# Expert rows taken one by one instead of in pairs, in a fused eight-block model kernel on one Trainium2 core

## Chip, cores and metric

One core of a Trainium2 chip runs the whole program in one launch. The metric is device time in microseconds (us), median of several runs. Three runs of the kernel before gave 3692.46, 3696.25 and 3700.17 us.

## The reference, cut to what matters

Three layers run on 512 tokens of width 1024, all in float32: a short-convolution mixer with a feed-forward part, a state-space mixer with a feed-forward part, and a hybrid layer (band attention beside a gated delta rule) that ends in a retrieval of single-neuron experts. The change concerns that retrieval alone. For each token, eight heads choose 16 of 16384 experts each, so 128 experts per token:

```python
u = expert_down[experts]              # 128 rows of 1024 per token
vv = expert_up[experts]
act = gelu(einsum("thkd,td->thk", u, hb))
out = einsum("thk,thkd->td", gates * act, vv)
```

## The kernel before

**Stages.** The first two layers and the first half (tokens 0 to 255) of the hybrid layer run first. Then the expert stage begins for the four chunks c = 0 to 3 of 128 tokens. While the experts of chunks 0 and 1 are worked on, the second half (f = 1) of the hybrid layer is computed beside them on the same engines, since chunks 2 and 3 need it.

**An expert row.** Tokens lie on the 128 partitions. "Row" n (n = 128c + s, 512 in all) is the s-th expert of each of the chunk's 128 tokens: one gather brings 128 x 2048 floats, 1 MB: `expert_down` in the left half and `expert_up` in the right half. `pool_gather` issues it on GpSimd's queue into a slot of `SLOTS`, after the row that had the slot before has been added (`added(prev[n])`). There are 7 slots (`NRING`) for rows 0 to 255 and 12 from there on, when memory of the finished hybrid layer is added.

**What is done with it.** Rows go in groups of `GG` = 2. `dve_dots` (VectorE, profile line L187) forms the dot with the tokens for each row of the group. `act_gelu` (ScalarE, L164, 128 x GG) applies Gelu to the group's dots; `dve_gate` (VectorE, L170, 128 x GG) multiplies by the gates; `act_diag` (ScalarE, L164, 128 x 128) writes a diagonal matrix for each row; `pe_add` (TensorE, L153) adds row times diagonal into two banks of PSUM with two 128x512 matmuls for a row (four records in the trace, since a float32 matmul shows as two). Some rows are added by VectorE instead (`own_add`, `dve_add`, L182, 128 x 1024): from s = 24 on, the rows with s % 4 = 1 in chunks 0 and 1, those with s % 16 = 9 in chunks 2 and 3. `dots` has 8 buffers of GG columns.

**Order of the work.** It is written out by hand. Each engine runs the same loop over groups. Between groups, `steps_of` places one piece of other work on each engine: a step of the second half's `main` (in chunk 0 two of them at every fourth group, and in chunk 1 one a group until it ends), and steps of `ranks` (the top-16 search of the next chunk on VectorE, L190 to L196), two a group in chunk 0. `main` goes on through attention, projections with the convolution of the delta rule, the inversion of triangular matrices for chunks 2 and 3 (`pe_invert`, `dve_invert`: the PE step and the VectorE step of one number wait for each other), the state's advance, the output projection, a norm, and the query projection. In iteration k (group k; rows 2k, 2k+1) the orders are:

```
VectorE:  dots(k)   gate(k-1)  own adds(k-1)  step k
ScalarE:  gelu(k)   diag(k-1)  step k
TensorE:  step k    add(k-1)
```

When the last row of a chunk has been added, `pe_finish` and `dve_finish` scale and add it to x, and `store` writes it.

Of the kernel before, what the change touches and what calls it, by code (L numbers as in the profile page):

```python
# [17 lines left out]
WORDS = 53200  # L18
LOW = 15944
BASE = LOW + 8192 + 6144  # L20
GG = 2

_COLS = [("c", 8), ("adab", 96), ("ng", 64), ("acw", 24), ("mcw", 128), ("mcb", 32), ("mng", 16),
         ("md", 16), ("c2", 8), ("adab2", 48), ("n1", 8), ("n2", 8), ("aog", 4), ("qg", 1), ("kg", 1),
# [195 lines left out]
def drive(*programs):  # L220

    live = list(programs)
    while live:
        live = [g for g in live if next(g, True) is None]


def build(nc, t, out):
    ctx = ExitStack()
    with ctx:
# [893 lines left out]
        def room(n):  # L1123
            a = t_at[0]
            t_at[0] += n
            assert t_at[0] <= WORDS - LOW, t_at[0]
            return tail[:, a:a + n]
# [21 lines left out]
        eidx = [room(128).bitcast(U32) for _ in range(2)]  # L1149
        dots = [room(GG) for _ in range(8)]  # L1150
        halo = tiles(room(36), 12)
# [48 lines left out]
        def wait_steps(n):  # L1200
            for _ in range(n):
                yield

        def some(steps, n):
            for _ in range(n):
                next(steps, None)
# [779 lines left out]
        def pe_tok(e, c):  # L1986
            for u in range(2):
                key = "htk", c, u
                o = ps.claim(key, QGB)
                e.wait_ge(*ps.vacant(key))  # L1990
                e.wait_ge(*t_h.at((5, c // 2, 7)))
                for k in range(4):
                    ins = e.tr(o[:, part[k]], H[:, 4 * u + k, part[c % 2]], ident)
                ins.then_inc(*tk_pe.tick((c, u)))
                yield
            yield

        def act_tok(e, c):
            yield
            for u in range(2):  # L2000
                e.wait_ge(*tk_pe.at((c, u)))
                if c > 1:
                    e.wait_ge(*g_dot.at(128 * (c - 2) + 127))
                e.act(htk[c % 2][:, 512 * u:512 * u + 512], ps["htk", c, u], ACT.Copy).then_inc(*ps.release(("htk", c, u)))
                yield
# [14 lines left out]
        def act_topk(e, c):  # L2020
            yield from wait_steps(31)
            e.wait_ge(*k_dve.at((c, "gate_in")))
            e.act(gates[c % 2], gates[c % 2], ACT.Exp).then_inc(*k_gate.tick(c))
            yield
# [68 lines left out]
        def pe_main(e, f):  # L2093
            yield from pe_norm(e, 4, f)
            yield from pe_qkv(e, f)
            yield from par(pe_att(e, f), both(wait_steps(16 * f), pe_dnp(e, f)))
            yield from par(pe_invert(e, 2 * f), pe_invert(e, 2 * f + 1), pe_aog(e, f))
            yield from pe_advance(e, 2 * f)
            yield from pe_advance(e, 2 * f + 1)
            yield from pe_post(e, f)  # L2100
            yield from pe_wo(e, f)
            yield from pe_norm(e, 5, f)
            yield from par(pe_pq(e, f), both(pe_tok(e, 2 * f), pe_tok(e, 1) if f == 0 else wait_steps(3)))
# [45 lines left out]

        GROUPS = 128 // GG  # L2150
        more = [over[:, 2048:4096], over[:, 4096:6144], over[:, 6144:8192], kv_mem[:, 0:2048], kv_mem[:, 2048:4096]]
# [9 lines left out]
        def own_add(n):  # L2161

            s = n % 128
            return s >= 24 and (s % 4 == 1 if n < 256 else s % 16 == 9)
# [15 lines left out]
        def dve_dots(e, c, grp):  # L2180
            n = 128 * c + GG * grp
            d = dots[(n // GG) % 8]
            e.wait_ge(*ps.done(("htk", c, 1)))
            for m in range(n - 8 * GG, n - 7 * GG) if n >= 8 * GG else ():
                e.wait_ge(*(g_own.at(m) if own_add(m) else g_diag.at(m)))
            for i in range(GG):
                s = SLOTS[slot_no[n + i]]
                e.wait_ge(*g_in.at((c, GG * grp + i)))
                e.ttr(s[:, 0:1024], s[:, 0:1024], htk[c % 2], d[:, i:i + 1]).then_inc(*g_dot.tick(n + i))
# [26 lines left out]
        def pe_add(e, c, grp):  # L2216
            for i in range(GG):
                s_i = GG * grp + i
                n = 128 * c + s_i
                if own_add(n):  # L2220
                    continue
                if s_i == 0:
                    for u in range(2):
                        ps.claim(("acc", c, u), (u,))
                        e.wait_ge(*ps.vacant(("acc", c, u)))
                e.wait_ge(*g_in.at((c, s_i)))
                e.wait_ge(*g_diag.at(n))
                for u in range(2):
                    ins = e.mm(ps["acc", c, u], diag[turn[n] % 8], SLOTS[slot_no[n]][:, 1024 + 512 * u:1536 + 512 * u],
                               s_i == 0, s_i == 127)  # L2230
                ins.then_inc(*g_mm.tick(n))

        def pe_finish(e, c):
            for u in range(2):
                o = ps.claim(("gB", c, u), HB)
                e.wait_ge(*ps.vacant(("gB", c, u)))
                e.wait_ge(*der_ok.at((5, "post")))
                for k in range(4):
                    ins = e.mm(o[:, part[k]], post(5, 4 * u + k).broadcast_to([128, 128]), ident)
                ins.then_inc(*f_pe.tick(("gB", c, u)))  # L2240
                o = ps.claim(("xo", c, u), HB)
                e.wait_ge(*ps.vacant(("xo", c, u)))
                for k in range(4):
                    ins = e.tr(o[:, part[k]], xT[:, 4 * u + k, 128 * c:128 * c + 128], ident)
                ins.then_inc(*f_pe.tick(("xo", c, u)))
# [42 lines left out]
        def before_rows(main, ranks):  # L2288

            for i in range(LEFT):  # L2290
                some(ranks, 1)
                if i < EARLY:
                    some(main, 1)

        def steps_of(c, grp, main, ranks):

            if c == 0:
                some(ranks, 2)
                some(main, 2 if grp % 4 == 3 else 1)
            elif c == 1 and next(main, True) is None:  # L2300
                pass
            else:
                some(ranks, 1)
# [3 lines left out]
        def pe_experts(e):  # L2307
            main = pe_main(e, 1)
            before_rows(main, iter(()))
            for g, (c, grp) in enumerate(ALL_GROUPS):  # L2310
                if grp == 0:
                    ranks = iter(()) if c == 3 else wait_steps(32)
                    late = pe_tok(e, 3) if c == 2 else iter(())
                steps_of(c, grp, main, ranks)
                next(late, None)
                if g:
                    pe_add(e, *ALL_GROUPS[g - 1])
                if g and grp == 0:
                    pe_finish(e, c - 1)
            pe_add(e, *ALL_GROUPS[-1])  # L2320
            pe_finish(e, 3)

        def act_experts(e):
            main = act_main(e, 1)
            before_rows(main, iter(()))
            drive(act_topk(e, 0))
            for g, (c, grp) in enumerate(ALL_GROUPS):
                if grp == 0:
                    ranks = iter(()) if c == 3 else act_topk(e, c + 1)
                    late = act_tok(e, 3) if c == 2 else iter(())  # L2330
                act_gelu(e, c, grp)
                if g:
                    act_diag(e, *ALL_GROUPS[g - 1])
                if c and grp == 4:
                    store(e, c - 1)
                steps_of(c, grp, main, ranks)
                next(late, None)
            act_diag(e, *ALL_GROUPS[-1])

        def dve_experts(e, ranks):  # L2340
            main = dve_main(e, 1)
            before_rows(main, ranks)
            drive(ranks)
            for g, (c, grp) in enumerate(ALL_GROUPS):
                if grp == 0:
                    ranks = iter(()) if c == 3 else dve_topk(e, c + 1)
                    late = wait_steps(3) if c == 2 else iter(())
                dve_dots(e, c, grp)
                if g:
                    dve_gate(e, *ALL_GROUPS[g - 1])  # L2350
                    dve_add(e, *ALL_GROUPS[g - 1])
                if c and grp == 1:
                    dve_finish(e, c - 1)
                steps_of(c, grp, main, ranks)
                next(late, None)
            dve_gate(e, *ALL_GROUPS[-1])
            dve_add(e, *ALL_GROUPS[-1])
            dve_finish(e, 3)
# [231 lines left out]
```

## Time and profile before

| | |
|---|---|
| median of 3 runs | 3696.25 us |
| the profiled execution's own time | 3689.87 us |
| its span, first to last instruction | 3687.9 us |
| TensorE busy (share of the span) | 3092.1 us (84%) |
| VectorE busy | 2120.4 us (57%) |
| ScalarE busy | 1129.1 us (31%) |
| mean granted TensorE clock | 0.93 |
| data moved | 797.76 MB, of it 536.90 MB in gathers |

PE is TensorE, DVE VectorE, ACT ScalarE, POOL GpSimd, PEld the weight load of TensorE. A share of the whole span is an average over stages with different limits, so it must be read stage by stage. "[1.98 <-DMA ...]" behind an instruction is the idle time of its engine before it and what ended it. The dot is two records, the product (1.21 to 1.23 us) and the read of its accumulator (0.08 us), so a count of x141 on its line means 70 rows.

### The profile page before, as it was taken

What the parts mean: (1) busy time and instruction counts of PE and PEld (TensorE: products, weight loads), DVE (VectorE), ACT (ScalarE), POOL (GpSimd) and SP (SyncE); (2) the same over time, 40 slices, a digit from 0 to 9 for tenths busy, and PEclk for the clock granted to TensorE, in tenths of its full rate; (3) what the DMA queues carried; (4) which work ended last, traced back from release to release, by engine and by line L of the source; (5) the groups of instructions that cost most, each with busy time, mean ns of one, the idle gap of its engine ahead of it and who ended that gap; (6) DMA issues with size and microseconds to landing.
All of it is one profiled execution on the core that took longest, in us unless ns stands there. A gap on an engine that the chain in (4) does not pass through costs nothing.

```text
span 3687.9 us, 33721 instructions
## 1 busy us (share of the span) xinstructions
PE 3092.1 (84%) x12138; PEld 2135.9 (58%) x12138; DVE 2120.4 (57%) x4048; ACT 1129.1 (31%) x2097; POOL 598.1 (16%) x540
## 2 busy tenths in 40 slices
PE   6989999798777989998889778887896667777777
PEld 4868887586555868886678634664572222223222
DVE  6654443776555354432552797685537868855554
ACT  3242222443444242223732344622221111111111
POOL 0000000000000000000000022233333344444442
PEclk9999999898888999998999888998998779999999
DMA  6534444242111434442203466878999999999997
GB/s 220 188 113 149 143 143 137 75 143 74 40 46 40 137 98 143 136 139 89 101 18 113 163 250 223 323 283 319 373 338 351 353 348 421 422 421 421 421 422 316
DMA packets 147540, 797.76 MB, mean 216 GB/s; under 512 B 16304, under 2 KB 18480, under 8 KB 81712
## 3 DMA queue, kind: packets, MB, share of 16 engines
q0 software_dynamic: 73728, 536.90, 37.0%
q1 hardware_dynamic: 69840, 251.69, 21.1%
q10 hardware_dynamic: 3808, 7.02, 0.5%
q8 instruction: 98, 1.61, 0.2%
q14 instruction: 66, 0.54, 0.0%
HBM read 793.46 MB, written 2.10 MB: 216 GB/s over the span
## 4 chain that ended last, share of the span: by engine, by line
PE 62%; DMA 19%; DVE 11%; ACT 4%; issue 3%; POOL 0%; DVEq 0%; SPq 0%; ACTq 0%
PE psum L153 61%; DMA tail<-in_experts,tail 19%; DVE tail L187 3%; ACT arena L164 2%; DVE arena L182 2%; DVE tail L170 1%; ACT L164 1%; DVE tail L182 1%; PE psum L158 1%; DVE tail L193 1%; DVE region L170 1%; ACT region L164 1%; DVE tail L190 1%; DVE rounded L182 0%; DVE arena L177 0%
## 5 line engine op out<-in xcount | busy, mean ns | idle before, releaser
L153 PE MATMUL psum<-tail,arena 128*128 128x512 f32 (+2 forms) x3652 | 1333.2, 519 | 336.6 <-ACT arena L164 309.1
L153 PE MATMUL psum<-rounded,rounded 128*128 128x512 f32 x5496 | 1293.6, 396 | 40.1 <-DVE rounded L182 27.3
L153 PEld LDWEIGHTS psum<-tail,arena 128*128 128x128 f32 x3652 | 713.8, 204 | 916.6 <-issue 852.4
L153 PEld LDWEIGHTS psum<-rounded,rounded 128*128 128x128 f32 x5496 | 1036.5, 190 | 280.1 <-issue 56.2
L187 DVE CUSTOM_DVE_ANT_0 tail<-tail 128x1024 f32<-128x1024 f32 x512 | 623.2, 1225 | 471.5 <-DMA tail<-in_experts,tail 469.2
L216 POOL DMA_INDIRECT tail<-in_experts,tail x512 | 578.0, 1129 | 1923.9 <-DVE tail L199 949.5
L170 DVE TENSOR_TENSOR rounded<-arena,rounded 128x1024 fp32r<-128x1024 f32 (+2 forms) x285 | 316.5, 1111 | 346.6 <-ACT rounded L164 346.5
L164 ACT ACTIVATE rounded<-arena 128x1024 fp32r<-128x1024 f32 (+2 forms) x317 | 291.8, 939 | 446.1 <-DVE arena L170 238.9
L164 ACT ACTIVATE tail<-tail 128x2 f32<-128x2 f32 (+1 forms) x288 | 64.1, 223 | 1131.9 <-DVE tail L187 1124.5
L153 PE MATMUL psum<-arena 128*128 128x1 f32 (+3 forms) x792 | 199.8, 378 | 81.4 <-ACT arena L164 48.7
L164 ACT ACT_TABLE_LOAD x180 | 230.9, 1283 | 11.7 <-PE psum L153 6.4
L164 ACT ACTIVATE arena<-psum 128x256 f32<-128x256 f32 (+2 forms) x210 | 97.3, 479 | 435.3 <-PE psum L153 435.0
L182 DVE SCALAR_TENSOR_TENSOR arena<-arena 128x512 f32<-128x512 f32 (+1 forms) x294 | 212.2, 724 | 21.7 <-ACT arena L164 10.9
L153 PEld LDWEIGHTS psum<-arena 128*128 128x128 f32 x792 | 127.9, 206 | 133.9 <-issue 82.6
L170 POOL TENSOR_TENSOR region<-region 128x256 f32<-128x256 f32 x24 | 19.9, 831 | 1130.4 <-DVE region L170 1130.4
L153 PE MATMUL psum<-tail 128*128 128x128 f32 (+4 forms) x888 | 139.2, 304 | 29.3 <-DVE tail L182 23.7
L164 ACT ACTIVATE arena<-arena,tail 128x128 f32<-128x128 f32 x446 | 154.6, 387 | 0.0
L153 PEld LDWEIGHTS psum<-tail 128*128 128x128 f32 (+2 forms) x888 | 109.2, 187 | 60.1 <-DVE tail L182 33.5
L170 DVE TENSOR_TENSOR arena<-psum,arena 128x512 f32<-128x512 f32 (+1 forms) x88 | 41.5, 475 | 168.2 <-PE psum L153 167.9
L182 DVE SCALAR_TENSOR_TENSOR arena<-psum,arena 128x511 f32<-128x511 f32 (+3 forms) x112 | 79.7, 712 | 71.3 <-ACT arena L164 43.8
L164 ACT ACTIVATE arena<-arena 128x512 f32<-128x512 f32 (+3 forms) x138 | 80.8, 598 | 91.6 <-DVE arena L170 29.3
L153 PE MATMUL psum<-region 128*64 128x128 f32 (+2 forms) x560 | 79.0, 362 | 33.7 <-DVE region L170 32.8
(82 smaller groups left out, 1556.2 us busy)
## 6 DMA issues: line engine op xcount, KB each, us to landing
arena<-in_ada SPq DMA_DIRECT2D x136, 512.0 KB, 3.9
arena<-in_fin SPq DMA_DIRECT2D x88, 512.0 KB, 4.2
arena<-in_win SPq DMA_DIRECT2D x56, 512.0 KB, 3.3
arena<-in_fout SPq DMA_DIRECT2D x32, 512.0 KB, 4.0
arena<-in_mxbc SPq DMA_DIRECT2D x32, 512.0 KB, 4.0
arena<-in_pq SPq DMA_DIRECT2D x32, 512.0 KB, 5.1
arena<-in_ain SPq DMA_DIRECT2D x24, 512.0 KB, 4.7
arena<-in_mz SPq DMA_DIRECT2D x16, 512.0 KB, 3.8
```

Of the source, the lines that this page charges most:

```text
L153: return self.e.matmul(o, a, b, start=start, stop=stop, skip_group_check=skip)
L158: return self.e.transpose(o, a, ident)
L164: return self.e.activation(o, a, func, bias=bias, scale=scale)
L170: return self.e.tensor_tensor(o, a, b, op)
L182: return self.e.scalar_tensor_tensor(out=o, in0=a, scalar=s, in1=b, op0=op0, op1=op1)
L187: return self.e.tensor_tensor_reduce(o, a, b, 1.0, 0.0, ALU.mult, ALU.add, total)
L190: return Unissued() if self.e is None else self.e.max(o, a)
L193: return Unissued() if self.e is None else self.e.max_index(o, m, a)
L216: return self.e.indirect_dma_start(out=o, out_offset=None, in_=table, in_offset=bass.IndirectOffsetOnAxis(ap=rows, axis=0))
```

## The change

`GG` becomes 1: a group is one row, there are 128 groups in a chunk, and Gelu and gate work on 128 x 1. The steps of the other work stay as many and in the same order: they are placed after every second group, so that one step still comes for two rows. `store` moves from group 4 to group 8, which is the same row. `dve_finish` stays at group 1, which is now row 1 rather than rows 2 and 3.

```diff
-GG = 2
+GG = 1
@@ pe_experts
-                steps_of(c, grp, main, ranks)
-                next(late, None)
+                if grp % 2:
+                    steps_of(c, grp // 2, main, ranks)
+                    next(late, None)
                 if g:
                     pe_add(e, *ALL_GROUPS[g - 1])
@@ act_experts
                 if g:
                     act_diag(e, *ALL_GROUPS[g - 1])
-                if c and grp == 4:
+                if c and grp == 8:
                     store(e, c - 1)
-                steps_of(c, grp, main, ranks)
-                next(late, None)
+                if grp % 2:
+                    steps_of(c, grp // 2, main, ranks)
+                    next(late, None)
@@ dve_experts
                     dve_add(e, *ALL_GROUPS[g - 1])
                 if c and grp == 1:
                     dve_finish(e, c - 1)
-                steps_of(c, grp, main, ranks)
-                next(late, None)
+                if grp % 2:
+                    steps_of(c, grp // 2, main, ranks)
+                    next(late, None)
```

For rows 2k and 2k+1 the orders are then:

```
VectorE:  dot(2k) gate(2k-1) own(2k-1)  dot(2k+1) gate(2k) own(2k)  step k
ScalarE:  gelu(2k) diag(2k-1)  gelu(2k+1) diag(2k)  step k
TensorE:  add(2k-1)  step k  add(2k)
```

`dots` is 8 columns in place of 16, so a dot waits for the diagonal of the row eight before it. 8 words less in front of the slots leave their number at 7.

## Rows read from the trace of the kernel before

**Rows 1.** Windows: stretch, length, busy of PE, PEld, DVE, ACT, POOL, clock, DMA share, GB/s.

```profile
2107.00:2245.00 138.00, 94.47 (x242) 43.93 (x241) 125.07 (x362) 58.34 (x111) 31.65 (x28) 0.81 0.68 254
2245.00:2392.00 147.00, 135.06 (x496) 90.40 (x494) 98.42 (x227) 82.30 (x144) 36.70 (x34) 0.92 0.77 285
2392.00:2496.00 104.00, 90.68 (x492) 66.87 (x493) 83.53 (x145) 25.54 (x55) 34.02 (x29) 0.93 0.79 295
2496.00:2537.00 41.00, 28.94 (x105) 17.11 (x104) 22.58 (x39) 7.05 (x21) 14.69 (x12) 0.83 0.87 324
2537.00:2608.00 71.00, 60.26 (x194) 37.65 (x193) 38.43 (x69) 15.38 (x34) 22.14 (x20) 0.93 0.87 339
2608.00:2650.00 42.00, 29.84 (x87) 14.86 (x85) 26.12 (x52) 13.43 (x33) 15.20 (x14) 0.92 0.93 354
2650.00:2773.00 123.00, 122.42 (x504) 85.82 (x505) 49.74 (x91) 26.51 (x91) 37.27 (x35) 1.00 0.93 347
2773.00:2985.00 212.00, 133.56 (x221) 51.51 (x221) 169.44 (x405) 30.54 (x98) 81.14 (x70) 0.80 0.94 349
2985.00:3035.00 50.00, 33.86 (x56) 13.04 (x55) 28.01 (x55) 5.42 (x21) 22.56 (x20) 0.77 0.94 350
3035.00:3358.00 323.00, 240.55 (x515) 96.83 (x514) 230.98 (x536) 52.31 (x190) 148.94 (x131) 0.95 1.01 422
```

**Rows 2.** Timeline, late chunk 1: one turn of the ring of slots.

```profile
2834.36 0.94 POOL L216 DMA_INDIRECT tail<-in_experts,tail  x1 [0.70 <-PE psum L153]
...
2837.84 5.11 PE L153 MATMUL psum<-tail,arena 128*128 128x512 f32 x8 [3.76 <-ACT arena L164]
...
2842.06 1.23 DVE L187 CUSTOM_DVE_ANT_0 tail<-tail 128x1024 f32<-128x1024 f32 x1 [1.98 <-DMA tail<-in_experts,tail]
...
2844.00 1.96 PE L153 MATMUL psum<-tail,arena 128*128 128x512 f32 x4 [1.05 <-ACT arena L164]
...
2846.23 0.94 POOL L216 DMA_INDIRECT tail<-in_experts,tail  x1 [2.07 <-PE psum L153]
```

**Rows 3.** Timeline, late chunk 1: gate and search step twice, an own add between.

```profile
2825.83 0.16 DVE L170 TENSOR_TENSOR tail<-tail 128x2 f32<-128x2 f32 x1
...
2827.62 1.21 DVE L187 CUSTOM_DVE_ANT_0 tail<-tail 128x1024 f32<-128x1024 f32 x1
...
2854.85 1.28 DVE L182 SCALAR_TENSOR_TENSOR tail<-tail 128x1024 f32<-128x1024 f32 x1
...
2893.79 1.23 DVE L187 CUSTOM_DVE_ANT_0 tail<-tail 128x1024 f32<-128x1024 f32 x1
...
2896.09 0.16 DVE L170 TENSOR_TENSOR tail<-tail 128x2 f32<-128x2 f32 x1
...
2898.55 1.21 DVE L187 CUSTOM_DVE_ANT_0 tail<-tail 128x1024 f32<-128x1024 f32 x1
```

**Rows 4.** Timeline, the inversion: starts of four-pair turns, and its parts.

```profile
2442.82 1.22 DVE L187 CUSTOM_DVE_ANT_0 tail<-tail 128x1024 f32<-128x1024 f32 x1
...
2445.19 1.28 DVE L170 TENSOR_TENSOR tail<-psum,tail 128x512 f32<-128x512 f32 x2
...
2445.87 3.67 PE L153 MATMUL psum<-tail,arena 128*128 128x512 f32 x8 [1.68 <-ACT arena L164]
...
2454.89 1.88 PE L153 MATMUL psum<-tail,arena 128*128 128x512 f32 x4
...
2456.62 3.73 PE L153 MATMUL psum<-tail 128*128 128x128 f32 x32
...
2463.63 1.95 PE L153 MATMUL psum<-tail 128*128 128x128 f32 x16
...
2495.69 1.22 DVE L187 CUSTOM_DVE_ANT_0 tail<-tail 128x1024 f32<-128x1024 f32 x1
```

**Rows 5.** Timeline, the end: the last rows.

```profile
3667.40 13.62 PE L153 MATMUL psum<-tail,arena 128*128 128x512 f32 x24 [2.97 <-ACT arena L164]
3670.44 1.23 DVE L187 CUSTOM_DVE_ANT_0 tail<-tail 128x1024 f32<-128x1024 f32 x1 [1.09 <-DMA tail<-in_experts,tail]
```

**Rows 6.** Timeline, attention: a one-column instruction of VectorE.

```profile
2149.89 0.15 DVE L176 TENSOR_SCALAR tail<-tail 128x1 f32<-128x1 f32 x1
```

## The prediction

> **What bounds the kernel now.** Over the whole span TensorE is busy most, but the stages have different limits, and the change touches only the time after the first gather (about 2107 us). So I cut that time into stretches with the windows view, at the changes of `main` that the timeline shows, and asked of each which engine has no idle time [rows 1]. From 3035 us on the DMA engines are full (share 1.01, 422 GB/s): a row is 1.0486 MB, so it takes 2.487 us, and no order of the engines helps. From 2107 to 2245 VectorE is full (125 of 138 us: attention and two search steps a pair). From 2245 to 2392 and from 2650 to 2773 TensorE is full (135 of 147, 122 of 123). From 2392 to 2496, the inversion, TensorE and VectorE are both near full (91 and 84 of 104): they overlap. From 2496 to 2650 and from 2773 to 3035 none is: VectorE has 169 of 212 us in the stretch from 2773, and the DMA engines move 349 GB/s where they can move 422.
>
> What bounds that last stretch is the ring of 7 slots [rows 2]. A gather issued at 2834.36 lands just before the dot at 2842.06; then gate, diagonal, add at 2844.00 for 1.96 us, and the freed slot is gathered into at 2846.23. This turn of 11.87 us serves 4 rows, as the slot freed is that of the first row of the pair before: row n is freed only behind the dot of row n+3. 11.87/4 is 2.97 us a row, against 2.487 for the DMA engines. The eight-record add (5.11 us for two rows) stretches the turn of a second row as much.
>
> **What the change does, part by part.** The profiled execution took 3689.87 us (span 3687.9), 6.4 us under the median of 3696.25; I sum differences against the profile and set them against the median.
>
> (a) **Late chunk 1, 2773 to 3035.** Row n is now freed behind the dot of row n+1, so a turn of about the same length serves 6 rows: about 2.0 us a row, no longer the bound. Next late is VectorE or the DMA engines. Two dots take 2.30 us back to back (2893.79 to 2896.09), gate and a search step over 256 columns 2.46 (to 2898.55); an own add is 1.28 every second pair, 0.64 a pair; the second gate adds about 0.1 [rows 3]. That is 5.5 us a pair. Gate and a search step over 128 columns take 1.79 (2825.83 to 2827.62), so 4.8 us, under the 4.97 of two rows of DMA [rows 3]. The 212 us at 349 GB/s are 70.6 rows, 35.3 pairs; 32 of them hold one of the search's 32 steps (16 over 128 columns, one that combines, 8 over 256, 6 that pick, one that ends). I take 16 pairs at 5.1, 14 at 5.5, the two odd ones at 6.2 and 6.5 and 3.3 without a step at 5: 188 us, saving 24. The 50 us after it are 16.7 rows at 350 GB/s, 41.5 us at full rate, saving 8.5. Of these 32.5 I take two thirds, -22, as some waits for landings stay in a fixed order. Bounds: -5 (the stretch behind the search alone gains, and in part) and -38 (no VectorE idle time from 2773 to 2985: 169 + 4 of gates, and the 8.5, less a wait or two).
>
> (b) **Output projection and norm, 2537 to 2650.** TensorE is idle 23 of 113 us while the DMA engines move 339 to 354 GB/s [rows 1]: it waits there for rows that came late. Earlier release gives a third back: -8 (bounds 0 and -15).
>
> (c) **The end.** The last dot starts at 3670.44, while TensorE adds from 3667.40 to 3681.0 in one run of 24 records, six rows, because the last two pairs become ready together [rows 5]. One by one, only rows 510 and 511 remain behind the last dot: add of 511 ends about 0.6 + 2 x 2.3 after 3671.7, near 3676.5. -4.5 (bounds -2 and -6).
>
> (d) **The inversion, 2392 to 2496.** Here the change adds a wait. On TensorE step k now stands behind the add of row 2k-1, whose diagonal needs VectorE's step k-1, then dot(2k), the gate and ScalarE. Before, step k stood in front of the adds and ran while VectorE did the two dots. What is queued behind that add is TensorE's step, and VectorE's step of the same number waits for that. In half of the pairs row 2k-1 is an own add (no add on TensorE) and the wait falls away. Working: for a pair with the wait, 1.15 (dot) + 0.1 + 0.6 (gate to add) + 1.88 (add) [rows 4] = 3.7 us until TensorE's step; a product step then delivers its halves after half of 1.95 or of 3.73 [rows 4], VectorE's masks (0.64 an operation, two or four of them) end at 6.3 or 8.75. For a pair without it VectorE's own work is 3.7 us, and with the step 5.0 or 6.3; at the double steps 8.0 or 9.5. Four pairs hold five steps of alternating kind: 26.9 in one turn, 32.0 in the next, mean 29.45. Before, two turns lasted from 2442.82 to 2495.69, 26.4 each [rows 4]. So +3.0 a turn, and the stretch is 3.94 turns: +12. Bounds: -5 if the waits for landings that it holds now also go, +30 if TensorE also gets slow (below).
>
> (e) **The state's advance, 2496 to 2537**, has the same kind of step, but its turn is bound by the ring too (324 GB/s, TensorE 29 of 41 us). The gain of (a) and the loss of (d) about cancel: +2 (bounds -3 and +6).
>
> (f) **Twice as many small instructions.** 256 more gates and 256 more Gelus. A gate of two columns takes 0.16 us, and an instruction on one column takes 0.15 [rows 3, 6], so halving the width halves nothing: 256 x 0.15 = 38 us more busy VectorE. The Trainium skill (VectorE: DVE Perf Modes, "The TRN2 errata") says that operations on SBUF pay a fixed cost for each instruction whatever their size; the rows agree. If the cost went by width, this term would be nothing; by the rule all 38 us are real work, and a slower kernel if VectorE were the bound throughout. By the windows it isn't [rows 1]: from 3035 to 3358 it is busy 231 of 323 us, less after that, and half of the gates lie there. It shows where VectorE is full: 18 pairs to 2245 at 0.12, +2 (bounds 0 and +5), and in (a) and (d), where it is counted. Gelu and Copy add no table load, as the order between two steps holds the same functions; ScalarE is busy at most 82 of 147 us in a stretch [rows 1].
>
> (g) **The TensorE-bound stretches** keep their work: the same matmuls. In projections and queries VectorE's and ScalarE's step uses what TensorE made one step earlier, so the diagonal of row 2k-1 is there some 5 us before TensorE comes to it. 0 (bounds -3 and +6). From 3035 on: 0, the queue of 12 slots hides 0.1 us a row. The shorter `dots` ring adds no wait: VectorE's dot of row n stands behind its own gate of row n-2, so row n-8's diagonal is long written. Sum: -22 - 8 - 4.5 + 12 + 2 + 2 + 0 = -18.5. 3689.9 becomes 3671.4, and 3696.25 becomes 3677.75, 3678.
>
> **The rivals.** *Same (release and coupling cancel).* (a) gives only -10, since VectorE's fixed order makes it wait for each landing in turn, and (d) and (e) cost 20: with the other terms -10 - 5 - 4 + 20 + 2 = +3, 3699, and down to 3689 with a little less. For it: VectorE is busy 80% there already. Against: the landing, not VectorE, ends its idle time in the turn shown [rows 2].
>
> *Slower (TensorE's lost overlap).* In the inversion TensorE falls idle 2 to 4 us in half of the pairs. In late chunk 1, where it idles between adds, the granted clock is 0.80, and eight records take 5.11 us where they take 3.67 in the inversion, at 0.93 [rows 1, 2, 4]. At that price each waiting pair's 4.7 us of TensorE work on the path becomes 6.7, and other stretches with same-number steps (attention's start, the norm's and the convolution's statistics) lose a little as well: (d) +30, (e) +6, (g) +10, (f) +4 against (a) -12, (b) -4 and (c) -4 give +30, and half of these losses +15: 3711 to 3726, 3716 as its middle. It decides as soon as a waiting pair costs over 3 us more than now rather than 1.6. The Trainium skill (TensorE: Matmul & The Clock Gate, "Why this matters for your kernels") wants no idle gaps between bursts of matmuls and so speaks for this rival; the row of late chunk 1 agrees.
>
> *The change does less than it says.* If the release of a slot isn't what bounds (a) but the latency of a gather, a row would stay at 2.97: no gain in (a), 3700. That is within the first rival.
>
> **How the numbers follow.** Forecast 0.55: 3678, own range 3650 to 3689. Cancelled 0.20: 3689 to 3704. Slower 0.25: 3716, from 3704. A measurement can tell about 0.2% (7 us) from no change. The range of 8 in 10: low 3652 (all gains near their ends: -38 -12 -5 +8 +1 +1 = -45), high 3712, which takes in the second case and about half of the third. Faster 0.57, same 0.18, slower 0.25.
>
> **What would show it.** Right: late chunk 1 above 400 GB/s, the rows of the 262 us from 2773 to 3035 done in some 240, gates 128x1 at 0.15 us, the last add within 6 us of the last dot. (d) right: the inversion 110 to 120 us long, with TensorE idle before adds, released by ScalarE. Wrong if: the inversion is over 130 us; the stretch after the queries still moves 350 GB/s; the time from DMA saturation to the end differs from 2.487 us a row; or the first 138 us grow by over 5.

## The result, and the profile after

The changed kernel takes 3630.27 us (median of 4 runs, 3627.36 to 3631.85) against 3696.64 us (4 runs, 3692.46 to 3700.17): a ratio of 0.982, 95% interval 0.9803 to 0.9837. That is 66 us faster, where 18 were forecast. The direction was right; the size, and the range's lower end of 3652, were not.

The profiled execution has a span of 3625.5 us. These are windows of the changed kernel (columns as in [rows 1]). They are cut at the events of the table below, so some of their ends lie up to 13 us off the places where [rows 1] was cut:

```profile
2098.00:2243.00 145.00, 104.72 (x283) 50.32 (x281) 129.41 (x385) 67.43 (x136) 43.35 (x37) 0.87 0.72 272
2243.00:2377.00 134.00, 127.55 (x489) 87.33 (x490) 99.80 (x242) 88.29 (x165) 33.51 (x30) 0.94 0.81 302
2377.00:2491.00 114.00, 92.15 (x499) 65.31 (x498) 83.60 (x159) 26.05 (x67) 37.01 (x32) 0.97 0.78 291
2491.00:2523.00 32.00, 24.84 (x96) 15.72 (x94) 20.25 (x39) 6.35 (x22) 11.76 (x9) 0.84 0.76 289
2523.00:2618.00 95.00, 80.63 (x265) 49.71 (x264) 56.98 (x116) 28.56 (x70) 36.19 (x31) 0.93 0.95 380
2618.00:2757.00 139.00, 136.18 (x540) 92.12 (x540) 65.15 (x142) 36.33 (x130) 46.98 (x42) 0.99 0.92 355
2757.00:2979.00 222.00, 147.44 (x278) 56.82 (x279) 194.87 (x490) 43.74 (x156) 110.49 (x89) 0.85 1.00 402
2979.00:3296.00 317.00, 240.91 (x487) 88.74 (x486) 231.41 (x595) 64.88 (x252) 138.43 (x127) 0.96 1.01 421
```

Two things are to be seen. Late chunk 1 (from 2757) now moves 402 GB/s, against 349 in the window of before that is cut at the same events:

```profile
2784.00:3037.00 253.00, 161.21 (x262) 61.76 (x260) 193.52 (x452) 34.74 (x116) 102.57 (x88) 0.80 0.94 349
```

And chunk 2 runs at the same rate as before (421 against 422). The table gives the time between the same events in five kernels, read from their timelines (the first gather; the last reciprocal of chunk 1's search; the transposes that open the inversion; the first product of the advance; the squares behind it; the norm's products; the query statistics; the finish of chunks 1 and 2; the end). In the changed kernel a chunk's finish comes two rows earlier in the order, so I moved its marks by 4.97 us, two rows of DMA. Each column is one execution. The time before the first gather, where all kernels do the same work, is not in the table: it is 2097.9 to 2108.5 us in the eleven traces, so a difference of a few us between two spans can come from there.

| stretch, us | before | changed | e1 | e5 | e4 |
|---|---|---|---|---|---|
| search and attention | 148.0 | 145.1 | 150.2 | 145.8 | 145.1 |
| projections | 147.1 | 133.9 | 148.6 | 138.4 | 124.1 |
| inversion | 104.2 | 114.5 | 106.7 | 184.7 | 95.2 |
| advance | 35.2 | 31.3 | 33.5 | 40.4 | 27.2 |
| output projection, norm | 102.6 | 95.8 | 102.4 | 108.4 | 93.8 |
| queries | 146.7 | 138.5 | 150.0 | 144.8 | 140.4 |
| late chunk 1 | 252.6 | 221.7 | 261.7 | 256.4 | 219.0 |
| chunk 2 | 322.8 | 322.8 | 324.1 | 322.7 | 324.0 |
| chunk 3 and end | 328.5 | 324.1 | 327.9 | 327.0 | 324.3 |

The changed kernel gains 31 us in late chunk 1, 13 in the projections, 8 in the queries, 7 in the output projection, 4 each in the advance and at the end, 3 in the first stretch, and loses 10 in the inversion. That is 60 of the 62 us between the two spans; the other 2 lie before the first gather. This timeline of it is late chunk 1, the place of [rows 2]:

```profile
2801.45 0.94 POOL L216 DMA_INDIRECT tail<-in_experts,tail  x1 [2.05 <-PE psum L153]
...
2801.74 1.23 DVE L187 CUSTOM_DVE_ANT_0 tail<-tail 128x1024 f32<-128x1024 f32 x1 [0.26 <-DMA tail<-in_experts,tail]
...
2804.32 0.94 POOL L216 DMA_INDIRECT tail<-in_experts,tail  x1 [1.93 <-PE psum L153]
...
2806.03 0.94 POOL L216 DMA_INDIRECT tail<-in_experts,tail  x1 [0.78 <-PE psum L153]
...
2807.56 1.68 POOL L216 DMA_INDIRECT tail<-in_experts,tail  x1 [0.59 <-DVE tail L182]
...
2811.40 0.94 POOL L216 DMA_INDIRECT tail<-in_experts,tail  x1 [2.16 <-PE psum L153]
...
2811.68 1.23 DVE L187 CUSTOM_DVE_ANT_0 tail<-tail 128x1024 f32<-128x1024 f32 x1 [0.25 <-DMA tail<-in_experts,tail]
```

Gathers start one by one, 1.5 to 3.8 us apart, and four rows take 9.94 us: 2.485 a row, the full rate of the DMA engines. In pairs there was mostly a hole of 5 to 7 us between bursts of gathers, and four rows took 11.87 [rows 2].

### The profile page after: what moved, and what is told of

It is laid out like the page before. It is cut to its first block, busy times and chain, and to the rows that moved or that the text cites. A ratio compares the mean times of both kernels' runs of the same rounds, so it can differ in the third digit from the quotient of the medians.

```text
span 3625.5 us, 34677 instructions
## 1 busy us (share of the span) xinstructions
PE 3074.4 (85%) x12138; PEld 2109.4 (58%) x12138; DVE 2134.3 (59%) x4304; ACT 1181.6 (33%) x2353; POOL 600.2 (17%) x540
## 4 chain that ended last, share of the span: by engine, by line
PE 61%; DVE 15%; DMA 14%; ACT 5%; issue 4%; POOL 0%; DVEq 0%; SPq 0%; ACTq 0%; POOLq 0%
PE psum L153 61%; DMA tail<-in_experts,tail 14%; DVE tail L187 4%; ACT arena L164 2%; DVE tail L170 2%; DVE arena L182 2%; ACT L164 1%; DVE tail L193 1%; DVE tail L190 1%; DVE region L170 1%; PE psum L158 1%; DVE tail L182 1%; DVE tail L196 1%; ACT region L164 1%; DVE tail L205 1%
## 5 line engine op out<-in xcount | busy, mean ns | idle before, releaser
L153 PE MATMUL psum<-tail,arena 128*128 128x256 f32 (+2 forms) x3652 | 1319.9, 510 | 306.6 <-ACT arena L164 282.2
L153 PEld LDWEIGHTS psum<-tail,arena 128*128 128x128 f32 x3652 | 690.3, 200 | 895.5 <-issue 835.4
L164 ACT ACTIVATE tail<-tail 128x1 f32<-128x1 f32 (+3 forms) x544 | 115.4, 213 | 978.2 <-DVE tail L187 812.6
L153 PEld LDWEIGHTS psum<-arena 128*128 128x128 f32 x792 | 127.8, 206 | 129.4 <-issue 80.3
L164 ACT ACTIVATE arena<-arena,tail 128x128 f32<-128x128 f32 x446 | 173.0, 388 | 1.1 <-issue 0.3
L170 DVE TENSOR_TENSOR tail<-tail 128x1 f32<-128x1 f32 (+5 forms) x555 | 135.7, 246 | 35.3 <-ACT tail L164 25.8
```

What stands on the lines that cost most here:

```text
L153: return self.e.matmul(o, a, b, start=start, stop=stop, skip_group_check=skip)
L164: return self.e.activation(o, a, func, bias=bias, scale=scale)
L170: return self.e.tensor_tensor(o, a, b, op)
```

## Experiments

Theory R: the gain is the earlier release of gather slots, row by row, and it is paid for by a tighter coupling of TensorE's steps to the rows. Rivals: the finer instructions themselves help (I); the order of adds against TensorE's steps is the gain (O); late chunk 1 is bound by a gather's latency and not by the ring (L). The kernel before, timed beside the experiments three times, took 3692 to 3693 us, and 3696.64 beside the changed kernel. So a difference between an experiment and the changed kernel (3630.27 us) is unsure by some 4 us, and the ratios, each to the kernel before timed beside it, are the safer comparison.

**e1: small instructions alone.** `GG = 1`, but in each loop rows go in the order of pairs:

```diff
@@ pe_experts (act_experts and dve_experts likewise)
                 if grp % 2:
-                    steps_of(c, grp // 2, main, ranks)
-                    next(late, None)
+                    continue
+                steps_of(c, grp // 2, main, ranks)
+                next(late, None)
                 if g:
+                    pe_add(e, *ALL_GROUPS[g - 2])
                     pe_add(e, *ALL_GROUPS[g - 1])
```

> The changed kernel's one-column Gelus and gates, but in the order of pairs on every engine: two dots, then the two gates and own adds of the pair before, then the step; two adds behind TensorE's step. It isolates the price of twice as many small instructions. Theory R (the gain is earlier release of the gather slots, row by row): nothing of the 66 us is kept, and the small instructions cost 2 to 10 us: 3697 to 3708. Rival I (finer instructions themselves help, by shorter waits between engines): under 3680.

Measured: 3701.86 us, ratio 1.0028 (1.0013 to 1.0044). Nothing of the gain is left, so rival I is out, and 256 more Gelus and gates cost 10 us (5 to 16 by the interval). The two traces lie further apart than the medians, 20 us: 9 of them are in late chunk 1, 3 in the queries, 3 before the first gather, 2 to 3 in the inversion and 2 in the first stretch. That the small instructions cost most where they lengthen the ring's turn fits this, but one pair of traces doesn't show it.

**e2 and e3: one slot less,** in pairs (e2) and one by one (e3).

```diff
-        NRING = (WORDS - LOW - t_at[0]) // 2048
+        NRING = 6
```

> The kernel before with 6 early slots in place of 7. Theory R: in pairs a turn of the ring then serves 3 rows and not 4, 11.87/3 = 3.96 us a row where the ring is the bound (some 85 rows of late chunk 1: +85 us), and more stretches become bound by it: +100 to +200 us in all, 3800 to 3900. Rival L (what bounds late chunk 1 is a gather's own latency or rate, not the ring): under +10 us.

> The changed kernel with 6 early slots in place of 7. Theory R: one by one a turn serves 5 rows, 11.87/5 = 2.37 us a row, still under the 2.487 of the DMA engines: +5 to +40 us on 3630, so 3635 to 3670, a quarter or less of what the same slot costs in pairs. If the release were no tighter in pairs than one by one, both lose the same.

Measured: e2 3872.54 us, ratio 1.0482 (1.0448 to 1.0516), so +180 us; e3 3657.03 us, 0.9907 (0.9873 to 0.9941), +27 us on the changed kernel. The windows of late chunk 1, of e2:

```profile
2914.00:3232.00 318.00, 165.59 (x256) 64.03 (x255) 194.37 (x451) 34.92 (x116) 103.58 (x88) 0.74 0.75 278
```

and of e3, to a row's finish like that of before:

```profile
2771.00:3007.00 236.00, 154.77 (x278) 58.54 (x279) 195.17 (x489) 43.39 (x156) 107.76 (x88) 0.83 0.97 379
```

In pairs the stretch grows from 253 to 318 us at 278 GB/s. That is 1.26 times, near the 4/3 of three rows a turn instead of four. Rival L falls. One by one it grows by 14 us. In pairs, every stretch from the first gather to the end of chunk 1 grows, and only from chunk 2 on, with 11 slots in place of 12, nothing does: first stretch 148.0 to 173.4 us, projections 147.1 to 172.5, inversion 104.2 to 127.8, advance 35.2 to 44.6, output projection 102.6 to 120.6, queries 146.7 to 166.6. So late chunk 1 has 66 us of the loss and the stretches before it 122: none of them was free of the ring.

**e4: TensorE's step in front of the add again.** Only the place of TensorE's step changes (and the finish of a chunk on VectorE, from row 1 to row 3, without which the two engines would wait for each other):

```diff
@@ pe_experts
-                if grp % 2:
+                if grp % 2 == 0:
                     steps_of(c, grp // 2, main, ranks)
@@ dve_experts
-                if c and grp == 1:
+                if c and grp == 3:
                     dve_finish(e, c - 1)
```

> The changed kernel, but TensorE's step k stands in front of the add of row 2k-1 again, as in the kernel before, and not behind it (the finish of a chunk on VectorE moves from row 1 to row 3). Theory R with the coupling of term (d): the inversion gets its overlap back, 104 instead of 114.5 us, the rest keeps its gain: 3615 to 3625. Rival O (part of the gain is that adds stand in front of TensorE's long steps, so that slots come free before the step): the projections and queries give back up to 21 us: 3635 to 3650.

Measured: 3599.38 us, ratio 0.9752 (0.9718 to 0.9785): 31 us less than the changed kernel (25 to 27 against the kernel before timed beside each), more than either theory gave. By the table 19 are in the inversion, now shorter than before the change, and 10 in the projections; the queries give back 2 and chunk 2 one. So the coupling costs about twice what I had for it, and not in the inversion alone. The waits view of the inversion, of the changed kernel:

```profile
DVE tail L170 <- PE psum L153: 23.4, 14, 4.2
...
PE psum L153 <- ACT arena L164: 14.6, 9, 3.3
```

and of e4:

```profile
DVE tail L170 <- PE psum L153: 6.3, 10, 1.6
...
PE psum L153 <- ACT arena L164: 2.3, 3, 1.1
```

VectorE's waits for TensorE's products fall by 17 us and TensorE's for diagonals by 12: these are the two ends of the chain that the step behind the add made. In the kernel before they were 3.7 and 3.1. The windows of e4, of its projections and its inversion:

```profile
2248.00:2372.00 124.00, 121.20 (x491) 83.62 (x490) 99.38 (x243) 87.67 (x164) 33.65 (x33) 1.00 0.89 335
2372.00:2468.00 96.00, 88.85 (x500) 65.60 (x499) 83.45 (x160) 26.46 (x68) 36.34 (x32) 0.96 0.89 334
```

**e5: the order alone, in pairs.** The kernel before with the adds of pair k-1 in front of TensorE's step k:

```diff
+                if g:
+                    pe_add(e, *ALL_GROUPS[g - 1])
+                if g and grp == 0:
+                    pe_finish(e, c - 1)
                 steps_of(c, grp, main, ranks)
                 next(late, None)
-                if g:
-                    pe_add(e, *ALL_GROUPS[g - 1])
-                if g and grp == 0:
-                    pe_finish(e, c - 1)
```

> The kernel before (pairs) with one thing changed: on TensorE the adds of pair k-1 stand in front of step k and not behind it. It gives pairs the other part of the change, the order of adds against steps, without single rows. Theory R: slots of a pair come free earlier by the length of TensorE's step, so the projections and queries gain (up to 20 us), but the inversion loses its overlap (+10 to +25) as VectorE's pair of dots and the gate now lie in front of each step: 3685 to 3705. Rival O (the order is most of the changed kernel's gain): 3640 to 3665.

Measured: 3780.37 us, ratio 1.024 (1.0217 to 1.0263), +87 us: a miss for both theories in size, and rival O is out in its sign. 80 of the 87 us are in the inversion. Its timeline there shows the chain in full:

```profile
2504.75 1.22 DVE L187 CUSTOM_DVE_ANT_0 tail<-tail 128x1024 f32<-128x1024 f32 x1
...
2505.89 1.22 DVE L187 CUSTOM_DVE_ANT_0 tail<-tail 128x1024 f32<-128x1024 f32 x1
...
2507.04 0.16 DVE L170 TENSOR_TENSOR tail<-tail 128x2 f32<-128x2 f32 x1
...
2507.80 3.75 PE L153 MATMUL psum<-tail,arena 128*128 128x512 f32 x4 [4.29 <-ACT arena L164]
...
2511.34 2.71 PE L153 MATMUL psum<-tail 128*128 128x128 f32 x16
...
2513.20 0.69 DVE L170 TENSOR_TENSOR tail<-psum,tail 128x512 f32<-128x512 f32 x1 [4.68 <-PE psum L153]
```

Two dots, gate, add, product, mask stand one behind the other, and each engine idles while the other works. The clock pays too: the window of that inversion shows 0.79, and an add of four records takes 3.75 us where [rows 4] have 1.88.

```profile
2388.00:2572.00 184.00, 121.24 (x498) 77.89 (x497) 83.67 (x144) 23.28 (x52) 29.56 (x32) 0.79 0.49 182
```

The projections do get 9 us shorter, as theory R had it from the earlier release. I had counted the coupling as one dot and one add; in pairs it is two dots and up to two adds, in every pair.

**e6 and e7: what bounds late chunk 1 now.** VectorE's own adds of every fourth row end at row 184, in the changed kernel (e6) and in e4 (e7):

```diff
-            return s >= 24 and (s % 4 == 1 if n < 256 else s % 16 == 9)
+            return s >= 24 and (s % 4 == 1 if n < 184 else s % 16 == 9)
```

> The changed kernel with VectorE's own adds of every fourth row ended at row 184 rather than 256 (every sixteenth from there on), so that 18 of its adds less 5 go to TensorE, in the stretch behind the queries. If VectorE is the bound of late chunk 1 once rows are freed one by one (5.5 us a pair by the sum of the prediction, over the 4.97 of the DMA engines, and busy 47 to 49 of 50 us in the trace): 13 adds of 1.28 us less, -8 to -15 us, 3615 to 3622. If the ring is still the bound, TensorE's later release makes it slower or changes nothing: 3628 to 3640.

> The two changes that gained or should gain, together: TensorE's step in front of the add of row 2k-1 (3599 us alone) and own adds of every fourth row only up to row 184. Theory R with VectorE as the bound of late chunk 1: 3585 to 3592. If not: 3597 to 3608.

Measured: e6 3625.29 us, ratio 0.9816 (0.98 to 0.9833), 5 us less than the changed kernel where 8 to 15 were expected, and with overlapping intervals (the ratios, 0.9816 and 0.982, are nearly the same), so no gain is shown; e7 3591.62 us, 0.9726 (0.9709 to 0.9744), 8 us less than e4, in the range that was expected (3585 to 3592), but with intervals that overlap too. The window of e6, from the query statistics to the finish of chunk 1:

```profile
2760.00:2968.00 208.00, 151.70 (x301) 56.35 (x301) 174.14 (x468) 46.94 (x167) 97.56 (x87) 0.94 1.01 418
```

Against the changed kernel's 216.7 us between the same events that is 9 less, at 418 GB/s: VectorE was what was next late there, but by little, as the DMA engines are full 9 us further on. Not all of it reaches the end of the run. The spans of the two traces differ by 3 us: against these 9 and 3 more in the queries, e6's trace is 4.6 us longer before the first gather, 2 in the output projection and 2 in chunk 2. In e7 late chunk 1 is 5 us shorter than in e4 (213.8 against 219.0).

**e8: is TensorE's work the bound of the projections?** e7 with seven more of VectorE's own adds, rows 39 and 43 to 63 (`or 36 <= n < 66 and s % 4 == 3`).

> The kernel of e7 with seven more rows added by VectorE (39, 43 to 63, those of the projection stretch), where TensorE is now busy 121 of 124 us at full clock and VectorE 99. If TensorE's work is the bound there, as the prediction held of the kernel before (where it was busy 132 of 147): 7 x 1.88 us less, -5 to -12 us on 3592, 3580 to 3587. If the order of VectorE's work is as tight, its 7 x 1.28 us eat it: 3590 to 3596.

Measured: 3593.99 us, ratio 0.9731 (0.971 to 0.9752): no gain. The window of its projections:

```profile
2253.00:2380.00 127.00, 114.01 (x467) 79.50 (x466) 106.91 (x249) 85.67 (x158) 37.80 (x35) 0.99 0.89 333
```

TensorE is busy 114 us instead of 121, VectorE 107 instead of 99, and the stretch is no shorter (127 against 124). So less work on TensorE doesn't shorten it, even from 98% busy, if VectorE gets more: VectorE's order is about as tight. The run can't say which of the two alone would bind, since both were changed.

**e9: e4 with six slots.**

> The kernel of e4 (one by one, TensorE's step in front of the add of row 2k-1) with 6 early slots in place of 7. Theory R: the release in it comes as early as in the changed kernel or, for an odd row, later by TensorE's step, so the lost slot costs as much as there (27 us, 3630 to 3657) or somewhat more: 3625 to 3645. If the step's place, not the release, were the gain of e4: it keeps its 31 us lead over the changed kernel with 6 slots, 3626. If later release of odd rows matters as much as the overlap won: 3645 to 3660.

Measured: 3631.38 us, ratio 0.9845 (0.9818 to 0.9873): 32 us over e4, against 27 for the same slot in the changed kernel (31 to 32 in the same way). So the kernel with the step in front needs its seventh slot no more than the changed one, and keeps a lead of 26 us with six.

## Why the prediction was wrong

- **(g) The TensorE-bound stretches, 0 forecast, -13 measured in the projections.** This is the step that failed. The prediction let the ring of slots bound only late chunk 1 and, in part, the output projection, and read TensorE's 135 of 147 us busy in the projections as a bound that the change doesn't touch. e2 shows what was there in its place: one slot less in pairs costs the projections 25 us, the first stretch 25 and the inversion 24, so the ring held them too. In the queries the reading was nearly right: they got 8 us shorter, but TensorE's idle time fell by 6 of these, and in the kernel before nearly all of that idle time lay outside the 123 us that [rows 1] shows full, in the edges that belong to (b) and (a). The waits view of before had a sign of it: for the projections it shows

```profile
DVE tail L187 <- DMA tail<-in_experts,tail: 33.8, 14, 9.1
```

 and in the changed kernel

```profile
DVE tail L187 <- DMA tail<-in_experts,tail: 3.8, 2, 3.0
```

 VectorE waited 34 us for landings, and 30 of these went. That this reached TensorE by way of VectorE's and ScalarE's steps is argued, not followed wait by wait; TensorE's idle time in the stretch fell from 15 to 6 us. Nor is busy time a fixed amount of work. The same matmuls are busy 132 us in the windows view of before,

```profile
2248.00:2395.00 147.00, 132.06 (x492) 89.23 (x490) 98.83 (x227) 83.75 (x146) 36.88 (x34) 0.93 0.79 293
```

 127.5 in the changed kernel and 121.2 in e4, where the granted clock is 1.00. Part of "full" was a slower clock behind idle gaps. e4 shows 23 us to be had there.
- **(a) Late chunk 1, -22 forecast, -31 measured.** The mechanism and the sum (-32.5) were right. The third that I took off for waits that stay was wrong (the measured stretch begins at 2784 and not at 2773): VectorE's waits for landings in the stretch fell from 53 to 20 us. e2 bears out the count of rows a turn (1.26 times where the count gives 4/3), e6 that VectorE and the DMA engines are next, close together. The bound of -38 was itself too near: the terms named for it, 39 us of VectorE's idle time and the 8.5, make 47.5, less a wait or two.
- **(b) -8 forecast, -7 measured** to the norm's products at 2637, and 3 to 5 us more to 2650, where the prediction cut; **(c) -4.5 forecast, -4.4 measured.** The last dot starts at 3613.08 and the last add ends at 3618.65, within 6 us.
- **(d) The inversion, +12 forecast, +10 measured,** but right by luck, as two errors cancelled: e4 puts the coupling at +19, and the release at -9, which I had only as a bound. The row that was forecast, TensorE idle before an add and released by ScalarE, is there:

```profile
2455.61 5.37 PE L153 MATMUL psum<-tail,arena 128*128 128x512 f32 x8 [2.23 <-ACT arena L164]
...
2460.82 3.73 PE L153 MATMUL psum<-tail 128*128 128x128 f32 x32
...
2462.80 1.29 DVE L170 TENSOR_TENSOR tail<-tail,psum 128x512 f32<-128x512 f32 x2 [4.23 <-PE psum L153]
```

 TensorE's step (2460.82) stands behind the add, and VectorE waits 4.23 us for its product. The clock share of the slower rival was wrong for this kernel (0.97 in the stretch), and right for e5.
- **(e) The advance, +2 forecast, -4 measured:** the release outweighed the coupling, as in (d).
- **(f) Small instructions, +2 beside what (a) and (d) held.** The first stretch came out 3 us shorter and not 2 longer; e1, which has the same instructions without the release, has it 2 longer. The gates take 0.156 us each at one column, as at two columns before and near the 0.15 forecast: this row is of the changed kernel's groups,

```profile
L170 DVE TENSOR_TENSOR tail<-tail 128x1 f32<-128x1 f32 x512 | 80.1, 156 | 21.4 <-ACT tail L164 21.4
```

 and in e1 the gates and Gelus cost 10 us of 3692 in all, so the Trainium skill's rule of a fixed cost per instruction (VectorE: DVE Perf Modes, "The TRN2 errata") holds in the row and was small in the sum.

Taking rows one by one with TensorE's step left in front, small instructions included, is worth 92 us (e4's span against before), where the prediction's gains add up to 35. The step behind the add takes back 29 (e4 against the changed kernel, by their spans), where it had 14. Both were there in the argument, each at less than half its size. The direction was right for the reason given; of the 48 us by which the total missed, the projections have 13, late chunk 1 9, the queries with their edges 8, the advance 6 and the first stretch 5; most of the rest lies before the first gather and between the profiled executions and the medians. None of the signs that it named for being wrong came up, since they watched the terms that held. Two smaller slips in its sums change nothing: 0.6 + 2 x 2.3 behind 3671.7 is 3676.9, and the middle of 3711 to 3726 is 3718.5.

## What to carry to other kernels

In a ring of buffers, count how many rows one turn of the ring serves: the release of a row behind the work on rows after it counts as buffers lost. With 7 slots the last slot was worth 180 us in pairs and some 30 one by one (e2, e3). What an eighth slot would give in pairs, no run shows. An engine that is busy nine tenths is not yet a bound: look at who waits for landings beside it, and at its clock. A run with one buffer less shows in one go which stretches hang on the ring; here it was all of them before chunk 2. When a wait moves in front of another engine's step, move the step too: e4, with the same instructions, gained 93 us where the change alone gained 66, and e7 (3591.62 us) has the lowest median of this study.

## What the runs showed of the hardware

- Gathers of 1.0486 MB run at 421 to 422 GB/s in chunk 2 with its 12 slots, 2.49 us each; with a ring of 6 slots in pairs (e2, late chunk 1) the core moved 278.
- TensorE's busy time for the same work in one stretch was 132, 127.5 and 121 us at mean granted clocks of 0.93, 0.94 and 1.00, and an add of four records took 1.88 us in one place and 3.75 in another (e5, behind 4.29 us of idle time): the granted clock is 1.00 in the first and 0.50 in the second, its two levels of 2.4 and 1.2 GHz. I had not expected that waits of up to 3.3 us for a diagonal would cost the changed kernel so little (0.97 in its inversion) and waits of up to 5.2 us e5 so much (0.79).
